# Context's latent projections in experts 0 and 1, in smaller blocks at later pieces of the weight ring

## What is computed

```python
aff = softmax(h @ w_router)                  # 256 tokens x 16 experts
g, idx = top_k(aff.T, 32)
he = silu(xe @ wg) * (xe @ wu)               # xe: 32 x 1024, wg and wu: 1024 x 2816
ye = (he @ wd) * g                           # wd: 2816 x 1024
```

```python
q  = rms_norm(hc @ w_dq, q_norm) @ w_uq      # 1024 -> 512 -> 8 heads x (128 + 64)
ckv = hc @ w_dkv                             # 1024 -> 256 + 64
kv = rms_norm(ckv[:, :256], kv_norm) @ w_ukv # 256 -> 8 heads x (128 + 128)
```

## Time and profile before

| | us |
|---|---|
| Median of 3 runs | 2432.94 |
| Lowest and highest run | 2430.75, 2435.43 |
| The profiled execution, its own time | 2430.89 |
| Its span, first to last instruction | 2429.1 |
| PE busy with matmuls | 2149.9 (89%) |
| VectorE busy | 690.4 (28%) |
| ScalarE busy | 221.7 (9%) |
| Experts 0 and 1 | about 219 to 393 |

### The profile page before, as it was taken

The page is one execution under the profiler, slowest core; times in us unless marked ns, Lnnn a source line. Parts: engine busy times, 40 slices in busy tenths (PEclk is TensorE's granted clock), DMA queues, the critical chain, the costliest instruction groups (busy, mean ns, idle before and its releaser), DMA issues.

```text
span 2429.1 us, 29545 instructions
## 1 busy us (share of the span) xinstructions
PE 2149.9 (89%) x12712; PEld 1164.1 (48%) x12712; DVE 690.4 (28%) x1469; ACT 221.7 (9%) x520; POOL 41.3 (2%) x109
## 2 busy tenths in 40 slices
PE   7989998879768888888888887998999999989998
PEld 6544453333323334334334342534659845646953
DVE  1232111210300100100100103002337865076876
ACT  1221110000100000000000000001320000060000
POOL 0000000000000000000000000000000003000000
PEclk9999999999999999999999899999999999999999
DMA  8898999999999999999999999998409465334550
GB/s 320 324 411 332 389 408 424 424 424 421 424 424 417 418 420 411 420 420 408 418 418 415 416 419 424 416 417 354 185 24 275 174 216 191 140 95 132 173 191 35
DMA packets 154819, 799.51 MB, mean 329 GB/s; under 512 B 15587, under 2 KB 71626, under 8 KB 101634
## 3 DMA queue, kind: packets, MB, share of 16 engines
q1 hardware_dynamic: 144504, 783.43, 80.1%
q10 hardware_dynamic: 10186, 14.16, 1.8%
HBM read 795.40 MB, written 7.19 MB: 330 GB/s over the span
## 4 chain that ended last, share of the span: by engine, by line
PE 62%; DMA 28%; DVE 4%; SPq 2%; issue 2%; ACT 2%; ACTq 0%; DVEq 0%
PE ps L293 12%; DMA ring<-in_mlp_w 11%; PE ps L2571 8%; PE ps L326 7%; PE ps L2582 6%; DMA ring<-in_w_down 6%; PE ps L2083 5%; PE ps L2051 5%; DMA ring<-in_w_up 4%; PE ps L2252 4%; DMA ring<-in_w_gate 4%; PE ps L2056 3%; SPq L224 2%; PE ps L2244 2%; DMA ring<-in_na_w_qkv 2%
## 5 line engine op out<-in xcount | busy, mean ns | idle before, releaser
L2051 PE MATMUL ps<-ring,xe 128*32 128x512 f32 x2016 | 287.5, 636 | 84.3 <-DMA ring<-in_w_up 42.4
L2083 PE MATMUL ps<-ring,expert_work 128*32 128x512 f32 x1408 | 253.6, 678 | 41.6 <-DMA ring<-in_w_down 30.5
L2056 PE MATMUL ps<-ring,xe 128*32 128x256 f32 x2016 | 200.0, 461 | 6.9 <-issue 6.9
L2083 PEld LDWEIGHTS ps<-ring,expert_work 128*32 128x32 f32 x1408 | 62.2, 119 | 196.1 <-issue 118.7
L2056 PEld LDWEIGHTS ps<-ring,xe 128*32 128x32 f32 x2016 | 70.2, 110 | 173.0 <-issue 172.9
L2051 PEld LDWEIGHTS ps<-ring,xe 128*32 128x32 f32 x2016 | 55.2, 112 | 198.1 <-DMA ring<-in_w_up 64.6
L2244 PE MATMUL ps<-hT,ring 128*128 128x256 f32 x512 | 114.9, 382 | 13.0 <-DMA ring<-in_mlp_w 13.0
L2252 PE MATMUL ps<-ring,c_qT 128*128 128x512 f32 x256 | 115.0, 602 | 11.3 <-DMA ring<-in_mlp_w 11.3
L2244 PEld LDWEIGHTS ps<-hT,ring 128*128 128x128 f32 x512 | 96.1, 190 | 35.5 <-DMA ring<-in_mlp_w 21.1
L2366 DVE TENSOR_TENSOR c_qT<-c_qT 128x512 f32<-128x512 f32 x16 | 11.1, 692 | 338.6 <-ACT c_qT L2316 338.6
L2124 DVE SCALAR_TENSOR_TENSOR expert_work<-expert_work,ps 128x512 f32<-128x512 f32 (+1 forms) x32 | 17.5, 548 | 253.2 <-ACT expert_work L2110 253.2
(11 more groups left out here) (523 smaller groups left out, 2561.5 us busy)
## 6 DMA issues: line engine op xcount, KB each, us to landing
ring<-in_w_gate SPq DMA_DIRECT2D x126, 1408.0 KB, 19.9
ring<-in_w_up SPq DMA_DIRECT2D x126, 1408.0 KB, 20.2
ring<-in_w_down SPq DMA_DIRECT2D x112, 1536.0 KB, 23.5
ring<-in_mlp_w SPq DMA_DIRECT2D x96, 1024.0 KB, 8.0
ring<-in_ada_w SPq DMA_DIRECT2D x32, 1536.0 KB, 10.2
ring<-in_na_w_qkv SPq DMA_DIRECT2D x20, 1024.0 KB, 15.2
ring<-in_w_in SPq DMA_DIRECT2D x8, 1536.0 KB, 16.6
ring<-in_w_down SPq DMA_DIRECT2D x16, 512.0 KB, 23.6
```

The lines of the kernel that those rows point to most:

```text
L2051: nc.tensor.matmul(ps[32 * j:32 * j + 32, UP if up else GATE, :], xe[:, k, :], w[:, :, 4 * j:4 * j + 4], start=(k == 0), stop=(k == KC - 1))
L2056: last = nc.tensor.matmul(ps[32 * j:32 * j + 32, REST, 256 * up:256 * up + 256], xe[:, k, :], two, start=(k == 0 and not up), stop=(k == K ...
L2083: last = nc.tensor.matmul(ps[32 * j:32 * j + 32, GATE if half else UP, :], hgT[:, at:at + 32], w[:, (c - c0) * D + 512 * half:(c - c0) * D ...
```

## The change

dq's pieces stand after (0, 10) and its two jobs run after (0, 10) and (0, 13). dkv's piece stands after (0, 15) and its two jobs run after (0, 17) and (0, 19), in the down stage. uq's pieces stay after (1, 3), and its ten jobs run as two, three, two and three after (1, 3), (1, 5), (1, 7) and (1, 9). ukv's pieces stand after (1, 11), and its twelve jobs run as six and six after (1, 11) and (1, 13). ScalarE and VectorE evict dkv's jobs at the head of the norms. Nothing is computed that was not computed before.

```diff
-        CTX_AFTER = {(0, 8): ("dq",), (0, 12): ("dkv",), (1, 3): ("uq",), (1, 10): ("ukv",),
+        CTX_AFTER = {(0, 10): ("dq",), (0, 15): ("dkv",), (1, 3): ("uq",), (1, 11): ("ukv",),
                      (4, 2): ("o0",), (4, 6): ("o1",), (4, 10): ("o2",)}
...
             def act_first(self, act):
                 self.run_t.ev(act, "act")
-                self.run_d.ev(act, "act")
+                self.run_d.ev(act, "act", 0, NT)
 
             def act_norm(self, act):
                 cq, ckv = self.buf["cq"], self.buf["ckv"]
+                self.run_d.ev(act, "act", NT)
                 self.run_d.finished(act)
...
             def dve_first(self, dve):
                 self.run_t.ev(dve, "dve")
-                self.run_d.ev(dve, "dve")
+                self.run_d.ev(dve, "dve", 0, NT)
 
             def dve_norm(self, dve):
                 cq, ckv, kpe, v = self.buf["cq"], self.buf["ckv"], self.buf["kpe"], self.v
+                self.run_d.ev(dve, "dve", NT)
                 self.run_d.finished(dve)
...
+        UQ_AFTER = [(1, 3), (1, 5), (1, 7), (1, 9)]
...
-                elif at == (0, 8):
-                    lat.pe_down(pe, 0, NT)
-                elif at == (0, 12):
-                    lat.pe_down(pe, NT)
+                elif at in ((0, 10), (0, 13)):
+                    lat.pe_down(pe, (i - 10) // 3, (i - 10) // 3 + 1)
+                elif at in ((0, 17), (0, 19)):
+                    lat.pe_down(pe, NT + (i - 17) // 2, NT + (i - 17) // 2 + 1)
                 elif at == (1, 1):
                     lat.pe_norm(pe)
-                elif at == (1, 3):
-                    lat.pe_q(pe)
-                elif at == (1, 10):
-                    lat.pe_kv(pe)
+                elif at in UQ_AFTER:
+                    n = len(lat.run_uq.jobs)
+                    r = UQ_AFTER.index(at)
+                    lat.pe_q(pe, n * r // 4, n * (r + 1) // 4)
+                elif at in ((1, 11), (1, 13)):
+                    n = len(lat.run_ukv.jobs)
+                    lat.pe_kv(pe, n * ((i - 11) // 2) // 2, n * ((i - 11) // 2 + 1) // 2)
```

## The result

The changed kernel takes 2448.89 us (median of 4 runs, 2446.91 to 2451.81) against 2432.68 us before (4 runs, one more than in the table above): 1.0073 of it, with an interval from 1.0061 to 1.0085. That is 16.2 us more, where 16.8 had been forecast. The profiled execution took 2446.91 us, 16.0 more than that of before.

The account below looks back on a forecast made before the run. The DMA's weight stream was taken as the bound. Holes of 1.0 + 6.8 + 4.9 + 11.3 + 2.2 = 26.2 us against 9.4 give +16.8: 2447.7 or 2449.7 us, range 2441 to 2457.

Parts of the forecast that it names:

- The bound: DMA weight stream, unbroken from 334 to 1570 us: lost transfer reaches the end; slower slices give back 2 us at most.
- First hole: DMA gap at the experts' start: 0.92 us more queued to move shrinks it from 1.95 to 1.0 us.
- dq: DMA hole in expert 0: piece 16 waits for dq's slot until 259.8; 6.8 us, before 4.95.
- dkv: New DMA hole in expert 0's down stage: the eighth w_down piece waits for dkv's slot; 4.9 us.
- uq: DMA hole in expert 1: piece 10, eight behind uq, waits for uq's last part; 11.3 us, before 2.54.
- ukv: DMA hole behind ukv in expert 1: none by 0.3 us, but low clock adds 2.54; taken as 2.2 us.
- Norms: Norms after dkv's last part: evictions queue behind them, up to 1 us of PE, costing nothing under uq's wait.
- uq alone: Rival: dq's and dkv's holes no larger than before's 6.9 us together, only uq's grows; +8.8, 2441.7 us; chance 0.14.
- Low clock in every part: Rival: dkv's and uq's parts also run at 1.2 GHz after waits, 2.54 us each; 2454.8 us; chance 0.12.
- Smaller blocks keep the stream full: Rival: splitting frees the ring often enough, the three holes close, 9.4 us come back; 2423.5 us; chance 0.07.

Follow-up runs that it names:

- e1: The changed kernel with uq's ten jobs in one block again after (1, 3), dq, dkv and ukv still split; 2437.08 us, 1.0026 of the kernel before.
- e3: The changed kernel with uq's weights in a tile of their own outside the ring, same order and parts; 2434.18 us, 1.0015 of the kernel before.
- e5: The changed kernel with uq's four parts after (1, 3), (1, 4), (1, 5), (1, 6); 2443.50 us, 1.0043 of the kernel before.
- e6: The changed kernel with uq in two parts, five jobs after (1, 3) and five after (1, 9); 2450.01 us, 1.0074 of the kernel before.
- e8: The kernel before with whole blocks later, but uq's weights cut by heads into halves, each freeing its own piece; 2425.08 us, 0.9970 of the kernel before.
- e7: The kernel before with four whole blocks later: dq (0, 11), dkv (0, 13), uq (1, 6), ukv (1, 13); 2427.13 us, 0.9977 of before.
- e4: The changed kernel's places with no block split: dq (0, 10), dkv (0, 17), uq (1, 3), ukv (1, 11); 2430.73 us, 0.9993 of the kernel before.
- e2: The kernel before with only uq's ten jobs split into four parts after (1, 3), (1, 5), (1, 7), (1, 9); 2442.52 us, 1.0045 of it.

## Why the prediction was right

*The bound.* The stream behind the experts' start is unbroken before and after, and the loss of 26.3 - 9.4 = 16.9 us in two experts moved the end by 16.0. The few slices below the full rate gave back less than 1 us. That the sum of the holes came out at 26.3 against 26.2 is in part luck: the terms are off by +0.8, 0, -1.3, +1.3 and -0.7 us, and these cancel. The steps that carry the result, the release by the last job and piece 10 of expert 1 eight places behind uq, are those that the runs show.

*First hole*: 1.0 forecast, 1.8 measured. It hardly shrank. PE started the experts 0.4 us later in this execution, which explains half at most. The other runs that start with this order (e1, e3, e5, e6) lose 2.0 to 2.1 us from 226 to 236, where the kernel before loses 2.1 us too, so the 0.92 us of extra transfer is not seen; why is not shown.

*dq*: 6.8 and 6.8. The release was forecast at 259.8, and the load went at 260.29.

*dkv*: 4.9 and 3.6. Its load had gone by 260.29 + 29.42 = 289.7, a microsecond earlier than forecast: pieces 16 and 17 took 5.48 us and not 6.38.

*uq*: 11.3 and 12.6. The landing of uq's second piece (T) was forecast at 315.9, and PE went on at 315.53; its work up to the release took 29.3 us and not 28.5. That 0.8 is the larger part of the difference; the other 0.5 is not explained. The restart was no slower: ukv's second piece came 14.7 us after the issue, as forecast. By the runs with uq alone (+10.4) and without the hold (-14) this is where most of the change lies.

*ukv*: 2.2 and 1.5. The low clock came, as taken: PE waited 6.38 us, the clock was 0.50 from 349.6 to 356.4, and again inside ukv's block after a wait of 1.74 us. The first of these cost nothing here, since PE waited for ukv's second piece afterwards. The second did: the 22 matmul instructions at 359.55 took 6.70 us, where 22 of the 32 in 7.55 would be 5.2: 1.5 us more, where 2.54 had been taken. Stretches of the changed kernel, columns of the earlier trace rows:

```profile
349.60:356.40 6.80, 4.62 (x28) 1.11 (x32) 0.00 (x0) 0.00 (x0) 0.00 (x0) 0.50 1.00 423
360.50:362.50 2.00, 2.00 (x7) 1.56 (x6) 0.24 (x1) 0.38 (x1) 0.00 (x0) 0.50 1.05 436
```

That there would have been no hole without it, by the 0.3 us of the forecast, is not shown. In e1 and e6 the rest of ukv's first part took 5.02 and 5.01 us, at clock 1.00, and 1.3 and 1.0 us were lost behind ukv all the same: in e1 ukv's second piece came 15.8 us after the issue and not 14.7, in e6 PE waited 1.39 us for an expert piece between the two parts. A margin of 0.3 us does not outlast a delay of a microsecond, and low clock is one such delay of several.

The Trainium skill, "Perfetto Trace Analysis", section Matmul Optimizations, says that PE's power follows its use, so that matmuls should run back to back in batches. In these runs that shows only through waits, and not after each: the clock fell to 0.50 after 6.38 us in the changed kernel and after 2.00 us in e5, and stayed at 1.00 after 2.97 us in e1. No run shows a loss from the division itself: with the slots not held (e3), four parts cost at most the 2.1 us by which that run is slower, and its holes at dq and dkv (6.7 and 3.5 us, 5.0 and none before), less the 2.4 of the uq hole that is gone, more than account for it.

*Norms*: up to 1 us forecast, and 1.5 measured (PE waited 2.36 us for VectorE before the scatter, where it was 0.9 before). It cost nothing, since PE waited for uq's weights afterwards.

*The rivals.* "uq alone" is out as a whole, for dq's and dkv's holes grew as summed (+5.0 us with uq whole). "Low clock in every part" did not come about in the changed kernel's profile, but the first of uq's parts ran at 0.50 in the run with half the hold. "Smaller blocks keep the stream full" was wrong for this change and half right as an idea: it needs pieces that are cut as the blocks are (e8).

## What to carry to other kernels

In a ring with an in-order loader, count for each piece the consumer's work from its arrival to its **last** reader, and compare it with the transfer time of the pieces that may be loaded meanwhile; the difference plus the dead time of a load is lost, however small the blocks are. On these runs such a sum is good to a microsecond or two for one hole. Splitting a block only helps if its operands are split the same way, so that every part frees what it read; otherwise insert nothing between the parts. When the producer is the bound over the rest of the kernel, place extra work after the consumer has worked off the pieces that lie in the ring, so that the loader has free slots to fill meanwhile. Here whole blocks one to three pieces later gained 5.5 us (e7), with dq's hole closed; other later places (e4) gained nothing that can be told, and the split blocks lost 16.

## What the runs showed of the hardware

A load into an empty queue has a dead time of 3 us or more here. The changed kernel's first load after its longest hole was issued at 344.84, and ukv's second piece, the fourth load from there, was there for PE at 359.5: 14.7 us, of which 2 x 3.39 + 2 x 2.47 = 11.7 are transfer at 425 GB/s, so 3.0 are dead. The same sum behind the uq hole gives 2.9 to 3.1 us in the kernel before, e2, e4 and e6, but 3.6 in e7, 4.0 in e1 and 4.5 in e5 (16.2 us from 341.90); why it differs is not shown.

One execution's stretches at 1.2 GHz fall elsewhere than another's. In the same part of the program uq's first matmuls took 5.42 us in one kernel and 7.35 in the next, which moved a hole of some 10 us by 2; in a row-by-row sum this is a term of its own, and these runs give no rule by which to foresee it.
